# Modulation tiles from a second queue, and the second down panel prepared later

## The reference

```python
for l in range(DEPTH):
    ada_ctx = silu_ctx @ w_ada[l] + b_ada[l]      # (1, 9 * 1024), 9 sections
    ada_lat = silu_c @ w_ada[l] + b_ada[l]
    ...
def trunk_layer(h, ada, l, ...):
    n = rmsnorm(h, norm_g[l, 0]) * (1 + sc0) + s0
    h = h + 0.5 * g0 * swiglu(n, w_ffn_up[l, 0], w_ffn_down[l, 0])
    n = rmsnorm(h, norm_g[l, 1]) * (1 + sc1) + s1
    h = h + g1 * token_mix(n)          # long convolution, attention, 2-D Fourier, gates
    n = rmsnorm(h, norm_g[l, 2]) * (1 + sc2) + s2
    h = h + 0.5 * g2 * swiglu(n, w_ffn_up[l, 1], w_ffn_down[l, 1])
```

## Time and profile before

| what | value |
|---|---|
| median of 3 runs | 3253.72 us (3248.50 to 3254.36) |
| profiled execution, its own time | 3249.3 us |
| its span, first to last instruction | 3247.5 us |
| mean granted TensorE clock in the span | 0.975 |
| VectorE busy | 2125.2 us, 65% |
| ScalarE busy | 1140.3 us, 35% |
| GpSimd busy (its DMA issues) | 47.9 us, 1% |
| moved by DMA | 408.90 MB, 126 GB/s |

### The profile page before, as it was taken

The page is one execution under the profiler, slowest core; times in us unless marked ns, Lnnn a source line. Parts: engine busy times, 40 slices in busy tenths (PEclk is TensorE's granted clock), DMA queues, the critical chain, the costliest instruction groups (busy, mean ns, idle before and its releaser), DMA issues.

```text
span 3247.5 us, 48659 instructions
## 1 busy us (share of the span) xinstructions
PE 3046.4 (94%) x19892; PEld 2956.6 (91%) x19892; DVE 2125.2 (65%) x3521; ACT 1140.3 (35%) x1820; POOL 47.9 (1%) x92
## 2 busy tenths in 40 slices
PE   7999999998999998899898899889989999999998
PEld 4999999988999998898898899889889999999998
DVE  7666666637555668686768686864375556675665
ACT  3422222314444333332443333333144443343432
POOL 0000000000000000000000000000000000000000
PEclk9999999999999999999999999999899999999999
DMA  7265543353123423333313333324532143122222
GB/s 303 89 235 217 217 164 117 126 228 130 69 73 133 172 79 111 117 104 130 111 59 124 104 117 119 114 91 154 214 108 85 69 146 142 65 92 79 91 66 72
DMA packets 89744, 408.90 MB, mean 126 GB/s; under 512 B 10050, under 2 KB 13570, under 8 KB 68915
## 3 DMA queue, kind: packets, MB, share of 16 engines
q1 hardware_dynamic: 70752, 323.52, 28.0%
q0 software_dynamic: 9504, 56.78, 4.6%
q10 hardware_dynamic: 9266, 25.50, 2.1%
HBM read 359.46 MB, written 46.30 MB: 125 GB/s over the span
## 4 chain that ended last, share of the span: by engine, by line
PE 70%; DVE 16%; issue 4%; DMA 4%; ACT 4%; SPq 0%; DVEq 0%; ACTq 0%
PE tile_psum L741 21%; PE tile_psum L748 10%; PE misc_psum L856 9%; PE tile_psum L1211 5%; PE misc_psum L860 4%; DMA w_ada<-in_w_ada 4%; PE tile_psum L702 3%; PE misc_psum L667 2%; PE tile_psum L1215 2%; PE tile_psum L667 2%; PE tile_psum L707 2%; DVE w_ada L2198 1%; PE tile_psum L856 1%; DVE h L2246 1%; PE tile_psum L1076 1%
## 5 line engine op out<-in xcount | busy, mean ns | idle before, releaser
L741 PE MATMUL tile_psum<-n_hi,whi 128*128 128x320 f32 x1536 | 352.7, 310 | 3.6 <-issue 2.2
L741 PE MATMUL tile_psum<-n_lo,whi 128*128 128x320 f32 x1536 | 350.7, 309 | 0.0
L2075 DVE TENSOR_TENSOR wlo<-raw,whi 128x2048 fp32r<-128x2048 f32 (+4 forms) x130 | 250.5, 1930 | 140.3 <-ACT whi L1482 138.2
L741 PE MATMUL tile_psum<-x_hi,whi 128*128 128x320 f32 x1300 | 299.5, 311 | 20.0 <-DVE h L2246 14.4
L741 PE MATMUL tile_psum<-x_lo,whi 128*128 128x320 f32 x1300 | 298.0, 310 | 0.0
L741 PEld LDWEIGHTS tile_psum<-n_hi,whi 128*128 128x128 f32 x1536 | 258.4, 189 | 5.8 <-DVE n_lo L2166 3.3
L1482 ACT ACTIVATE whi<-raw 128x2048 fp32r<-128x2048 f32 (+4 forms) x130 | 209.4, 1617 | 145.1 <-DMA raw<-in_w_down 44.2
L741 PEld LDWEIGHTS tile_psum<-n_lo,whi 128*128 128x128 f32 x1536 | 258.7, 189 | 0.0
L1211 PE MATMUL tile_psum<-n_hi,whi 128*128 128x320 f32 x768 | 237.4, 320 | 10.9 <-ACT gate_out L1970 10.4
L2246 DVE SCALAR_TENSOR_TENSOR h<-tile_psum,ada_t,h 128x320 f32<-128x320 f32 (+2 forms) x408 | 154.2, 433 | 137.3 <-PE tile_psum L748 133.7
L856 PE MATMUL misc_psum<-n_hi,whi 128*128 128x320 f32 x648 | 198.7, 317 | 45.8 <-DVE hidden L2357 45.8
(11 more groups left out here) (383 smaller groups left out, 6433.7 us busy)
## 6 DMA issues: line engine op xcount, KB each, us to landing
w_ada<-in_w_ada SPq DMA_DIRECT2D x128, 512.0 KB, 5.4
raw<-in_w_up SPq DMA_DIRECT2D x72, 512.0 KB, 4.1
raw<-in_w_up SPq DMA_DIRECT2D x34, 1024.0 KB, 4.9
raw<-in_w_gate SPq DMA_DIRECT2D x24, 1024.0 KB, 4.9
raw<-in_w_down SPq DMA_DIRECT2D x29, 768.0 KB, 4.4
whi<-table_keep SPq DMA_DIRECT2D x20, 1024.0 KB, 4.7
wlo<-table_keep SPq DMA_DIRECT2D x20, 1024.0 KB, 6.9
g_keep<-gate_out POOLq DMA_DIRECT2D x48, 320.0 KB, 2.5
```

Source lines behind the costliest of these rows:

```text
L741: pe.matmul(tps[:, t.s, m, 0:TH], blk(p, m * n + k)[0], (hi, lo)[b][:, k, tok], start=k == 0 and b == 0, stop=False)
L2075: ins = dve.tensor_tensor(lo_at(r, n)[:, 0:w], raw_at(r, n)[:, 0:w], hi_at(h_, n)[:, 0:w].bitcast(F32), ALU.subtract)
```

## The change

Tiles 74 to 143 of the modulation weights (all that the first FFN doesn't use) are no longer requested by SyncE. GpSimd requests them in one loop on its own queue, after the mixer of layer 0, each as soon as the tile two before it has been used; they have semaphores of their own. In `fast_up` the rounding and the splitting of the second down panel move from the middle of the last group to behind the last hidden rows. This is the diff, whole but for its context.

```diff
+ADA_LATE = ADA_EARLY + sum(ADA_PLAN[0, 0])
...
+        ada_late = [sem(f"ada_late_in{k}") for k in range(2)]
...
                     t = tiles_in[0]
-                    if t == DEPTH * ADA_TILES:
+                    if t == ADA_LATE:
                         return
...
+                    if l == 0:
+                        pool.wait_ge(y_done, KT)
+                        for t in range(ADA_LATE, DEPTH * ADA_TILES):
+                            pool.wait_ge(ada_used, t - 1)
+                            pool.dma_start(adaw[:, t % 2, :], w_ada[t]).then_inc(ada_late[t % 2], 16)
...
                     if q + 1 < n:
                         fast_group(g + 1, 2)
-                    else:
-                        round_panel()
                     keep_p5(g)
                     keep_u2(g)
...
                 hidden_hi(n - 1, slice(TH, T))
+                round_panel()
...
-                        w, arrived = adaw[:, t % 2, :], ada_in[t % 2]
+                        w, arrived = adaw[:, t % 2, :], (ada_in if t < ADA_LATE else ada_late)[t % 2]
...
                     if q + 1 < n:
                         fast_low(g + 1, 1)
                         fast_low(g + 1, 2)
-                    else:
-                        split_panel()
                     ada_step(plan[q])
...
                 for j in range(2):
                     hidden(n - 1, slice(j * TH, (j + 1) * TH))
                     hidden_lo(n - 1, slice(j * TH, (j + 1) * TH))
+                split_panel()
```

## The result

| | before | changed |
|---|---|---|
| time, median (lowest to highest) of 4 runs each | 3251.11 us (3247.24 to 3254.36) | 3155.35 us (3150.92 to 3161.57) |
| ratio, 95% interval | | 0.9707 (0.9686 to 0.9729) |
| profiled execution: own time, span, granted clock | 3249.3, 3247.5 us, 0.975 | 3153.97, 3152.1 us, 0.984 |

The changed kernel is faster by 95.8 us; 92 were predicted, and 3161 us.

What follows compares the result with a forecast made beforehand. TensorE, busy 3046 of 3247.5 us, was taken as the bound, improvable only through holes and slow clock. 86.5 + 8.7 - 3 = 92 us off the median 3253.72 gave 3161; likeliest range 3146 to 3176, 8 in 10 3143 to 3192.

Steps and rivals of the forecast that it cites:

- Tiles on GpSimd's queue: 70 tile requests leave SyncE's queue; landing in 5.5 us, no tile waited for; 86.5 us less in six chunks.
- Rival 1: Loads on GpSimd's queue land late, up to 10.8 us; down stages lose 24 us: 3185 us, chance 0.12.
- Rival 4: Slower: GpSimd's queue lands tiles so late (14.3 us breaks even) that down stages lose more: 3306 us, chance 0.04.
- Rival 3: No change, 3254 us: the wait was for DRAM, not for the queue; chance 0.03.
- the chunks of A and B: Six seven-product runs: A1-A3 in layer 0's second FFN, B1-B3 in layer 1's first; 102.5 us too much. C1-C3: last FFN, tile-free.
- 12.6 us of holes: TensorE idle time expected to stay in the six tile-carrying chunks: 9.3 first sums, 1.7 A3's start, 1.6 last groups.
- 3.4 of slow clock: Slow-clock time in us expected to stay in the six tile-carrying chunks, since some holes near 2 us stay.
- 28.7 us: Excess TensorE busy time in the six tile-carrying chunks before, put down to the clock falling to 1.2 GHz behind holes.
- Rival 2: Tiles are there, but VectorE and ScalarE work together doesn't fit the group; 27 us stay: 3188 us, chance 0.14.
- The second panel: Rounding and split moved behind the last hidden rows close the hole at ScalarE's copies: 8.7 us less in C.
- The down stages: Four stages with tiles: the later panel split delays updates of `h`, 0.6 to 1.0 us each, 3 us more.
- case 5: Better: clock holds in every chunk and updates find their slack, 3155 us; chance 0.67 together with the forecast.

Runs made afterwards that it cites:

- one tile of cover: Changed kernel, but GpSimd requests a tile only when the one just before it is used, not two before: 3238.17 us, ratio 0.9945.
- plan-and-order kernel: Changed kernel with one tile per chunk group, a single tile first in each down stage, P1's copy before the first panel's rounding: 3139.81 us, ratio 0.9646.

## Why the prediction was right

**Tiles on GpSimd's queue.** The bound was read rightly: the late thing was the request. The timeline of GpSimd in the changed kernel, its first three tile requests in A1 (idle before, and what it waited for), with VectorE's last use of the tile before the second:

```profile
1283.56 0.53 POOL L1469 DMA_DIRECT2D w_ada<-in_w_ada  x1 [9.32 <-DVE w_ada L2204]
...
1303.60 1.22 DVE L2204 SCALAR_TENSOR_TENSOR w_ada<-w_ada,c_rows 128x1024 f32<-128x1024 f32 x1
...
1305.12 0.53 POOL L1469 DMA_DIRECT2D w_ada<-in_w_ada  x1 [21.03 <-DVE w_ada L2204]
1329.77 0.53 POOL L1469 DMA_DIRECT2D w_ada<-in_w_ada  x1 [24.11 <-DVE w_ada L2204]
```

The page's DMA issues (count, KB each, median us to landing):

```profile
w_ada<-in_w_ada POOLq DMA_DIRECT2D x70, 512.0 KB, 4.2
...
w_ada<-in_w_ada SPq DMA_DIRECT2D x58, 512.0 KB, 6.4
```

Each request now stands right behind VectorE's last use (0.3 us after its end at 1304.82), in place of 48 us after it, and lands in 4.2 us by the median where I took 5.5. Rival 1 (late landings) is refuted: VectorE waited for none of these tiles. Rival 4's mechanism exists, as the kernel with one tile of cover shows, but its landing time of 14.3 us was never near (the longest of all 128 tiles took 9.2). Rival 3 (the queue changes nothing) is refuted twice: by the result, and by the tiles moved up within SyncE's queue, which were not waited for either. The Trainium skill, "DMA: Bandwidth & Descriptors", section "Issuing engines are not separate DMA queues", says that transfers run on the same DMA engines whoever issued them, and the traces agree: the same 70 tiles land in 4.3 us from SyncE in the kernel with tiles one step earlier and in 4.2 from GpSimd. The time of issuing, the only thing that this section of the Trainium skill says is saved, is not what was saved here (an issue takes 0.33 us from SyncE by the median, 0.53 from GpSimd): that was the standing behind other requests' waits. By the figures of the Trainium skill, "SBUF — State Buffer", section "SBUF: two separate sides", I had estimated a landing of 8 us. The trace has 4.2 with VectorE busy for 60 to 72 of 77 to 82 us, so the lock did not show. The Trainium skill ties the lock there to VectorE instructions in a mode that takes both ports, and I had not asked whether those of this kernel use it; no run here shows that.

**Term by term, the chunks of A and B.** Predicted to remain were 12.6 us of holes and 3.4 of slow clock over 463.5, which makes 479.5; the sum is 477.1. The first sums of five chunks kept the 8.1 us that I had allowed, and the last groups of A3 and B3 their 1.6. A3's first group kept 1.64 where I had 1.7:

```profile
1526.85 0.38 PE L858 MATMUL misc_psum<-n_hi,whi 128*128 128x320 f32 x1 [1.64 <-DVE hidden L2363]
```

B3's first group, which I left as it was, got a new hole of 1.38 of the same kind, because it too has two tiles. That I came out at 12.6 for 12.7 all the same is luck: I had counted 1.2 us for slower starts as holes, and the trace has them as busy time. My 77.25 for a chunk without holes was misread too: C1 had a hole of 2.4 us and a slow start of 0.23 behind it, and A1 now shows 77.02. With that, no slow clock at all is left of the 28.7 us (PEclk 1.00 in all six), where I had left 3.4. The longest hole in them is now 2.13 us, and before it was 5.0.

**VectorE's room.** I had 2.3 us for a tile; 2.34 were measured. Rival 2 (no room in a group) is refuted by the chunk with a tile in each of six groups and no hole. Where the room does run out is two tiles in one group, 9.53 + 2 x 2.34 = 14.2 of 12.32 us, and that is what A3 and B3 begin with.

**The second panel.** 8.7 us in C were predicted, 9.15 measured. The mechanism stands on the last group of A1 (compare):

```profile
1337.64 0.44 ACT L1651 ACTIVATE hidden<-misc_psum 128x320 f32<-128x320 f32 x1 [1.08 <-PE misc_psum L862]
1339.39 0.44 ACT L1641 ACTIVATE hidden<-misc_psum 128x320 f32<-128x320 f32 x1 [1.32 <-PE misc_psum L862]
```

ScalarE waits for TensorE at each copy, and no longer for the panel's place: nothing stands in front of them. The kernel with the panel alone shows the rest: 16.0 us less in A and B, where the same hole was.

**The down stages.** Predicted were 3 us more in the four stages behind A1, A2, B1 and B2; measured are 164.5 - 160.4 = 4.1. After A1:

```profile
1352.35 1.76 DVE L2081 TENSOR_TENSOR wlo_more<-raw_more,whi 128x1536 fp32r<-128x1536 f32 x1 [0.89 <-ACT whi L1489]
1354.03 1.01 DVE L2252 SCALAR_TENSOR_TENSOR h<-tile_psum,ada_t,h 128x320 f32<-128x320 f32 x2
...
1362.70 0.56 PE L743 MATMUL tile_psum<-x_hi,whi 128*128 128x320 f32 x2 [0.50 <-DVE h L2252]
```

And the stretch of that stage:

```profile
1349.33:1390.62 41.29, 39.62 (x269) 39.10 (x268) 36.70 (x65) 9.88 (x12) 3.17 (x6) 1.00 0.35 115
```

The split now stands in front of the first update, and TensorE waits 0.50 us at the second pair, for which I had 0.6. The whole stage is 0.77 us longer (41.29 against 40.52). In the four stages these new waits are 3.0 us, what I had; the other 1.1 is busy time, 158.6 us against 157.5, the slower starts behind them, which I had left out. That the waits come from the tiles around the update is what the plan-and-order kernel shows, where all four are gone.

**The sum** of these places: A and B -88.9, C -9.15, down stages +4.1, that is -93.9 of the span's -95.4. The other 1.5 I did not trace. The total, 95.4 us for 92, is nearest to case 5 (3155 us), but only half of case 5 happened: the clock held in every chunk, and the updates did not find their slack.

## What to carry to other kernels

When a consumer waits for a transfer, first measure from "buffer free" to "requested" and only then from "requested" to "landed": here 48 us against 5.5, so that a queue was worth 78 us, with landings that hardly changed. An in-order queue that serves two consumers makes one wait for the other's buffers. Moving the tiles forward in it was worth 41 us and made the panels late; a queue of their own was worth some 75. After the large wait is gone, spread side work so that each group keeps a margin on the engine that does it: here that was worth another 19 to 31 us for a table of numbers and one swapped line (15 and 28 between profiled executions).

## What the runs showed of the hardware that was not expected

The clock came back wholly in the chunks: the six had PEclk between 0.93 and 0.98 before and 1.00 after, though holes up to 2.1 us are still in them. In the kernel before, the product of L856 behind a hole of 4.0 to 5.0 us took 0.60 or 0.61 us (as at 1344.32 in the earlier trace rows, and from there to 1348 the granted clock is 0.59); behind the holes up to 2.1 us of the changed kernel it takes 0.38 or 0.39. Between the runs of one program the time goes roughly with the granted clock: the plan-and-order kernel took 3128.75 us at 0.986, 3140.33 at 0.983, 3139.29 at 0.982 and 3143.26 at 0.980. So a difference of 5 us between two such kernels can't be read from medians of four. TensorE's idle time is of more help, but not exact either: 137.7 and 135.5 us in the two profiles of the changed kernel, most of it one wait for `h`.

Waits of VectorE that fall where its work is dense cost nearly their own length in all, but in two ways: 79.3 us of waiting in the one-tile-cover kernel made 51.8 us of holes in TensorE, and behind them TensorE was busy 33.4 us longer for the same products, at a clock of 0.972 in place of 0.984. VectorE is idle for a third of the span, and that absorbed only a third of its waits.
